# Two pairs of half-wide constant matmuls behind the first two slots of each feed-forward and mixer stage

## The reference

```
for l in range(DEPTH):
    mod = (c_act @ ada_w[l] + ada_b[l]).reshape(bsz, 3, 3, D_MODEL)
    h = _modulated_norm(x, norm_g[l, 0], mod[:, 0, 0], mod[:, 0, 1])
    x = x + MACARON_WEIGHT * mod[:, 0, 2][:, None, :] * _swiglu(h, ffn1_w_in[l], ffn1_w_out[l])
    h = _modulated_norm(x, norm_g[l, 1], mod[:, 1, 0], mod[:, 1, 1])
    mix = _token_mixer(h, positions, ...)
    x = x + mod[:, 1, 2][:, None, :] * mix
    h = _modulated_norm(x, norm_g[l, 2], mod[:, 2, 0], mod[:, 2, 1])
    x = x + MACARON_WEIGHT * mod[:, 2, 2][:, None, :] * _swiglu(h, ffn2_w_in[l], ffn2_w_out[l])
return _rms_norm(x, final_norm_g)
```

## Time and profile before

| | |
|---|---|
| median of 3 runs | 1367.28 us (1366.84 to 1370.79) |
| the profiled execution | 1372.02 us |
| its span, from first to last instruction | 1370.2 us |
| TensorE, matmuls busy | 1299.3 us (95%), 13038 of them |
| VectorE busy | 937.9 us (68%) |
| ScalarE busy | 634.4 us (46%) |
| GpSimd busy | 241.9 us (18%) |
| DMA | 298.27 MB, mean 218 GB/s |

### The profile page before, as it was taken

The page is one execution under the profiler, slowest core; times in us unless marked ns, Lnnn a source line. Parts: engine busy times, 40 slices in busy tenths (PEclk is TensorE's granted clock), DMA queues, the critical chain, the costliest instruction groups (busy, mean ns, idle before and its releaser), DMA issues.

```text
span 1370.2 us, 30166 instructions
## 1 busy us (share of the span) xinstructions
PE 1299.3 (95%) x13038; PEld 1264.5 (92%) x13038; DVE 937.9 (68%) x1332; ACT 634.4 (46%) x913; POOL 241.9 (18%) x265
## 2 busy tenths in 40 slices
PE   2999999999889999999999999999988999999998
PEld 1999999988779999999999999998977999999998
DVE  6766667677756776665677776677776478767655
ACT  2544335475624455333364434448564343643443
POOL 1233341011020001332004331000102000123300
PEclk9999999999999999999999999999999999999999
DMA  9987874716103746777658887752440175577762
GB/s 362 352 284 278 301 266 167 290 49 215 63 4 122 301 178 247 260 283 256 246 201 320 291 303 268 286 217 90 159 151 4 69 274 197 192 275 294 277 220 95
DMA packets 65137, 298.27 MB, mean 218 GB/s; under 512 B 9217, under 2 KB 10241, under 8 KB 47746
## 3 DMA queue, kind: packets, MB, share of 16 engines
q1 hardware_dynamic: 65026, 296.69, 59.7%
HBM read 295.62 MB, written 1.05 MB: 217 GB/s over the span
## 4 chain that ended last, share of the span: by engine, by line
PE 83%; DVE 8%; ACT 4%; DMA 2%; issue 2%; DVEq 1%; SPq 0%; ACTq 0%
PE PS L1447 23%; PE PS L1449 23%; PE PS L1448 23%; DVE wl L872 2%; PE PS L1548 1%; PE PS L1472 1%; PE PS L1916 1%; PE PS L1473 1%; PE PS L1476 1%; PE PS L1465 1%; PE PS L1702 1%; PE PS L1905 1%; ACT wh L549 1%; DMA raw<-in_ada_w 1%; DVE raw L958 1%
## 5 line engine op out<-in xcount | busy, mean ns | idle before, releaser
L872 DVE TENSOR_TENSOR wl<-raw,wh 128x1024 fp32r<-128x1024 f32 (+1 forms) x400 | 471.8, 1219 | 293.9 <-ACT wh L549 293.7
L549 ACT ACTIVATE wh<-raw 128x1024 fp32r<-128x1024 f32 (+1 forms) x400 | 396.8, 1039 | 489.6 <-PE PS L1449 435.4
L1447 PE MATMUL PS<-h_hi,wh 128*128 128x256 f32 x2064 | 579.5, 281 | 10.0 <-DVE wl L872 4.8
L1448 PE MATMUL PS<-h_lo,wh 128*128 128x256 f32 x2064 | 574.6, 278 | 0.0
L1449 PE MATMUL PS<-h_hi,wl 128*128 128x256 f32 x2064 | 574.5, 278 | 0.0
L1447 PEld LDWEIGHTS PS<-h_hi,wh 128*128 128x128 f32 x2064 | 388.1, 188 | 15.3 <-issue 10.2
L1448 PEld LDWEIGHTS PS<-h_lo,wh 128*128 128x128 f32 x2064 | 389.2, 189 | 0.2
L1449 PEld LDWEIGHTS PS<-h_hi,wl 128*128 128x128 f32 x2064 | 389.2, 189 | 0.0
L1449 PE MATMUL PS<-hid_hi,wl 128*128 128x256 f32 x704 | 196.1, 279 | 0.0
L1447 PE MATMUL PS<-hid_hi,wh 128*128 128x256 f32 x704 | 196.1, 278 | 0.0
L1448 PE MATMUL PS<-hid_lo,wh 128*128 128x256 f32 x704 | 196.1, 278 | 0.0
(11 more groups left out here) (293 smaller groups left out, 1435.8 us busy)
## 6 DMA issues: line engine op xcount, KB each, us to landing
raw<-in_ffn_w_in SPq DMA_DIRECT2D x88, 1024.0 KB, 5.6
ada_w_ring<-in_ada_w SPq DMA_DIRECT2D x154, 512.0 KB, 5.0
raw<-in_mix_w_in SPq DMA_DIRECT2D x46, 1024.0 KB, 6.1
raw<-in_ffn_w_out SPq DMA_DIRECT2D x44, 1024.0 KB, 5.6
raw<-in_branch_w SPq DMA_DIRECT2D x8, 1024.0 KB, 9.3
raw<-in_mix_w_out SPq DMA_DIRECT2D x8, 1024.0 KB, 4.8
raw<-in_ada_w SPq DMA_DIRECT2D x6, 512.0 KB, 10.9
raw<-in_mix_w_in SPq DMA_DIRECT2D x4, 512.0 KB, 3.7
```

Of the source, the lines that this page charges most:

```text
L549: nc.scalar.activation(wh[:, s % 2, h * n:(h + 1) * n], raw[:, s % 4, h * n:(h + 1) * n], ACT.Copy).then_inc(*one("w_hi"))
L872: V.tensor_tensor(wl[:, s % 2, h * n:(h + 1) * n], raw[:, s % 4, h * n:(h + 1) * n], wh[:, s % 2, h * n:(h + 1) * n].bitcast(F32), ALU.sub ...
L1447: M(out, wh[(slice(None),) + wsl], rhs_h, start=start, stop=False, skip_group_check=True)
L1448: M(out, wh[(slice(None),) + wsl], rhs_l, start=False, stop=False, skip_group_check=True)
```

## The change

A new helper, `settle`, issues four matmuls: the weights are 64 columns of ones, the moving operand is the identity matrix (128 columns), the results go to 64 partitions each of PSUM bank 7, lower half, upper half, and once more. The results are not read. It is called behind `first_pair` in the feed-forward and in the mixer, so six times in the program, 24 matmuls.

```
+            def settle():
+
+                for _ in range(2):
+                    for r in (slice(0, 64), slice(64, P)):
+                        M(PS[r, 7, 0:P], ones[:, 0:64], ident, start=True, stop=True, skip_group_check=True)
+
             def norm(l, n, inc=one, wide=P):
...
                         if j:
                             first_pair(s0, 0, f * 2 * KD, l)
+                            settle()
                         continue
...
                 first_pair(ATT_IN, 0, KD, l)
+                settle()
                 for s in range(ATT_IN + 2, RW_IN):
```

## The result

The changed kernel takes 1378.77 us (median of 16 runs, 1369.43 to 1387.40). The kernel before, run beside it, takes 1375.21 us (median of 16 runs, 1357.14 to 1379.61). The ratio is 1.0084, with a 95% interval of 1.0055 to 1.0114. That ratio leaves out runs more than 1.5% above the fastest of their kernel, and the kernel before has one run at 1357.14 that puts this bound at 1377.5, so five ordinary runs fall out of it; the plain means are 1372.8 and 1378.9 us, a difference of 6.1 ± 2.0 us (standard error). The prediction was 1356.2 us, faster. The profiled execution took 1376.50 us (span 1374.7, clock 0.999) against 1372.02 before.

What follows compares the result with a forecast made beforehand. TensorE's wide products were taken to bound the kernel, their pace set at each run's start. Two slow stages made fast, −13.2, plus insertions, +2.1, gave −11.1 us: 1356.2 us from the 1367.28 median, range 1353 to 1370.

Steps and rivals of the forecast that it cites:

- eight places: Wide products directly behind half-wide matmuls, lines 1827 and 1758 of the earlier trace: 6 of 8 at 113 ns.
- T: The experiments' theory against the prediction: an insertion exchanges the paces, s slow long runs becoming 4 - s, for 0.80 us each.
- the price: Time one insertion adds on TensorE where nothing hides it: 0.52 us, 2.1 us for the four feed-forwards.
- the base: The unchanged kernel's time to which the gain was carried over: median 1367.28 us.
- The cover in the mixers: TensorE already waits there for the third slot's split, so both mixer insertions were taken to cost 0.
- The suppliers keep up: With all four feed-forwards at the fast pace, splits and DMA would not come late; nothing was seen to.
- The formula in s: Change in time with s of the four feed-forward stages slow afterwards: 6.6 × (s − 2) + 2.1 us.
- Rival (b): Pace belongs to the stage, not its entry; insertion only paid: 1369.4 us; chance 0.12 with other ways to s = 2.
- Rival (c): Half-wide pairs drop all four feed-forwards into the 118 ns pace: +15.3, 1382.6 us; chance 0.13 together with s = 3.
- Rival (a): One feed-forward stage stays or becomes slow, or only one was slow in timed runs: −4.5, 1362.8 us; chance 0.20.

Runs made afterwards that it cites:

- e6: The changed kernel unaltered, run once more on a second chip beside the kernel before: 1370.0 us, ratio 0.9947.
- e9: The kernel before plus two half-wide pairs in the two mixers alone, none in the feed-forwards: 1377.68 us, ratio 1.0054.
- e12: The changed kernel without the mixers' insertions, two pairs in the four feed-forwards alone: 1373.96 us, ratio 1.004.
- e1: The kernel before plus two half-wide pairs ahead of each single input slot of the feed-forwards, 80 places: 1434.81 us, where before took 1363.98.
- e10: The changed kernel with one half-wide pair instead of two at all six places: 1365.21 us, ratio 0.9954 to the kernel before.
- e5: The changed kernel with one pair instead of two in the four feed-forwards and nothing in the mixers: 1372.28 us, ratio 0.9967 to the kernel before.
- e8: The kernel before plus three half-wide pairs ahead of each of the 80 feed-forward input slots: 1441.37 us.
- e3: The kernel before plus one full-width single-precision matmul ahead of each of the 80 feed-forward input slots: 1395.61 us, where before took 1363.98.
- e13: Second profile, no new edit, of the kernel with one pair in the four feed-forwards and none in the mixers: 1359.93 us.
- e15: Second profile, no new edit, of the kernel with one pair at all six places: 1388.92 us.
- e11: The kernel before, unchanged, as a run of its own against itself: 1373.18 us, ratio 1.0014.

## Why the prediction was wrong

**The step that failed: what the edit does to the pace.** The prediction took it that wide products settle at the fast pace behind half-wide matmuls, and its chance of 0.55 for four fast stages rested on a count of eight places that looked only at the pace behind. For the two stages of layer 1, which were fast already, the forecast needed a fast pace to stay fast, and none of the eight places shows that. Here is the place of the earlier trace rows once more, from further ahead:

```profile
429.90 0.28 PE L1449 MATMUL PS<-h_hi,wl 128*128 128x256 f32 x1
...
430.61 0.28 PE L1449 MATMUL PS<-h_hi,wl 128*128 128x256 f32 x1
430.82 1.53 PE L1827 MATMUL PS<-cst,hstat 128*64 128x128 f32 x24
432.28 0.39 PE L1447 MATMUL PS<-h_hi,wh 128*128 128x256 f32 x1
```

Six intervals from 429.90 to 430.61 are 118 ns each: the entry was slow, and so it was at 1094.56. At the other two head spreads (353.12 and 1015.71) the products ahead were slow too, with 0.79 and 0.80 us of idle time between. The four places of line 1758 stand, with the pair of line 1755 ahead of them, behind 0.51 to 0.74 us of idle time. So two of the eight are like the edit's places, and they turned slow into fast, as T has it.

Nor were the eight of one kind. A single-precision matmul leaves two records, and a merged row begins where the window was cut: the `x14` of the earlier trace rows is part of 24 records, twelve matmuls, six pairs, and the `x4` of the earlier trace rows is one pair. The program's own order said "x4" for the four new matmuls; four records in the trace were two. Measured instead: two pairs turned the pace at 6 of 6 places of the changed kernel, 6 of 6 in e6, 2 of 2 in e9, 4 of 4 in e12 and 80 of 80 in e1. With one pair in place of two the time would have come nearer to the forecast (e10 is at −8.7 ± 2.2 us and e5 at −4.4 ± 1.8, for −11.1 forecast), but not by its reasoning: a third of the slow entries stayed slow.

In the medians the miss of 22.6 us (1378.77 against 1356.2) adds up: 13.2 for two slow stages where none was forecast, 1.5 for the price, and 7.9 for the base (1375.21 against 1367.28). That the timed runs had two slow stages in the mean is read from the profiles only.

**The price.** 0.52 us was worked out and 0.80 measured, for the same reason: 0.32 from the earlier trace rows is one pair, and the second adds 0.22, as e8 shows once more. The end of the half-wide stretch was counted right (0.22 for the first interval). The cover in the mixers, 0.54 and 0.68 us in all, was too short for 0.79, which costs 0.36 us together. Sum over six places: 3.6 instead of 2.1 us. The Trainium skill has a reason for a price, in "TensorEngine Tiling (Array Packing)", section "Key Properties": changing the tiling mode drains TensorE. It gives no number; the trace has 0.21 us in and 0.20 out, and e3's full-width matmul, which changes no mode, costs 0.23 us where the half costs 0.58. The long first interval behind (0.22) is no mark of the mode, for e3 has one of 0.20 as well.

**The base.** Three runs (median 1367.28) passed for the kernel's time; 16 gave 1375.21, and over all comparisons the kernel before spans 1357.14 to 1391.98. The prediction saw the 4.7 us between the profiled execution and the median and named a slow stage as its possible cause, but then took the number of slow stages as fixed. It is drawn in each execution: in the 18 profiles of this study none to three of the four first pairs came out slow. Ordered by size, the runs of before on the third chip at full clock stand in groups, 1357.15, then 1363.63 to 1365.35, then 1369.4 to 1373.6, then 1377.7 to 1380.7, and one at 1388.78. From group to group it is some 7 to 9 us, which fits about one slow stage (6.6 us) each.

**What held.** The pace of a long run is settled at its start and kept for 1488 products (the windows above have no other lengths than 168.6 to 168.8 and 175.3 to 175.4 us, as forecast). The suppliers keep up with four fast stages: e5, e10 and e13 show no wait for a split in them. The formula in s held with its price mended. Rival (b) named s = 2, +2.1 us; the changed kernel's profile has s = 2, though not by that mechanism, for (b) assumed that the insertion does nothing to the pace. Its counterpart in the Trainium skill, "TensorE: Matmul & The Clock Gate", section "Back-to-back issue gap", is narrower than the prediction has it: N/2.4 + 2.5 ns (109 ns for 256 columns, an estimate) is given there for an isolated matmul, and for a stream in which each matmul loads its weights, as here, the section gives about 81 ns at 128 columns and 131 ns at 512, with none at 256. For streams too it has one spacing for a length; every profile here has two for 256 columns, 113.3 and 117.8 ns. Rival (c), that a fast stage can be made slow, is what happened at two of the four stages; it had the right price, 6.6 us a stage, and the wrong reason (a place with its own outcome, instead of an exchange). Rival (a), one slow stage, is what e6's profile shows, by the same exchange.

**Still open.** Why the first pairs start at one pace or the other, and whether they are slow more often on one chip (11 of 16 on the second) than on another (16 of 32 on the third). What the two paces are. And e5's gain: with 2.75 slow entries and a third of them staying, 0.57 us a place, the sum is −9.8 us, and −4.4 ± 1.8 was measured. The clock, below, explains little of it: the runs of e5 with a mean clock of 0.998 or more (5) lie 3.9 ± 3.0 us under those of before (15).

## What to carry to other kernels

When identical stages have two lengths, ask first whether the outcome is drawn anew in each execution: profile the unchanged kernel several times before building on one profile, and take its time from a dozen runs. Before calling places in a trace the same, compare the state ahead of them as well as the one behind, and count instructions in the program, not records in the trace. To learn what an inserted instruction does to a state, put it in 80 places of one run: each is a throw of its own, and the law shows at once where a dozen timed executions show only a mean.

## What the runs showed of the hardware

- Two paces of 128x256 fp32r matmuls at one granted clock, 1.00 (the 2.4 GHz level): 113.3 and 117.8 ns, kept for 1488 matmuls (168.65 and 175.25 us). One full-width matmul of 128 columns (fp32r, 0.12 us, or single precision, 0.23 us) or two half-wide pairs (0.80 us) exchange them, 240 places of 240, and two pairs did so at 18 of 18 further places. One pair (90 places without idle time), one half and three pairs (76 each) never spoiled the fast one. Not every interruption exchanges: the twelve single-precision matmuls of latent attention's scores, directly behind wide products, were entered 26 times slow and 10 times fast in the 18 profiles, and the pace behind was slow each time.
- The two halves of a half-wide pair start 6 to 7 ns apart, and one half alone costs what both do.
- The clock drops in some executions. Windows of all engines in e5, layer 1's mixer (behind POOL's count come the granted clock, the DMA share and GB/s), and the idle time ahead of it on TensorE's timeline:

```profile
905.00:910.00 5.00, 2.85 (x20) 2.65 (x19) 4.70 (x6) 3.49 (x5) 0.00 (x0) 0.86 1.02 420
910.00:915.00 5.00, 5.00 (x26) 5.00 (x25) 3.45 (x6) 0.00 (x0) 0.00 (x0) 0.50 0.88 302
915.00:920.00 5.00, 5.00 (x29) 5.00 (x29) 0.00 (x0) 0.00 (x0) 0.00 (x0) 0.62 0.98 405
```

```profile
907.51 0.33 PE L1531 MATMUL PS<-wh,h_hi 128*128 128x128 f32 x1 [2.15 <-DVE wl L872]
```

  0.50 is the 1.2 GHz level. It lasted 10.2 us, behind an idle time of 2.15 us for a split whose weights came late, and that mixer took 289.4 us against 284.0 in the changed kernel's profile. e9, e10 and e15 have such a stretch at nearly the same place. On the third chip, runs of before with a mean clock under 0.998 took 1376.9 us (16 of them), the others 1371.1 (19). (On the second chip it was 1380.1 against 1372.9.) The mean clock was that low in 24 of 58 runs of before and in 21 of the 48 runs of e5, e9, e10 and e11, though in none of the 40 runs of the changed kernel, e6 and e12, the kernels with two pairs in the feed-forwards. I expected the mixers' insertion to be the cause; e9, which has it, was low in 6 of 12, and e12, which lacks it, in none. What keeps the clock up there is open.
